# Keeping the running sum of a depthwise convolution in two PSUM banks, with the sample rows' products moved ahead of the taps

## What is computed

```python
h = xn @ w_in + b_in
a, gate = jnp.split(h, 2, axis=-1)
u = a * jax.nn.sigmoid(gate)
upad = jnp.concatenate([hist, u], axis=1)          # hist: 30 earlier rows (zero for the prompt)
y = depthwise_conv(upad, w_dw) + b_dw              # 31 taps, each channel by itself
y = jax.nn.silu(layernorm(y, ln_g, ln_b))
out = y @ w_out + b_out
```

## Time and profile before

| what | value |
| --- | --- |
| time, median of 3 runs | 3446.14 us (3438.42 to 3453.7) |
| span of the profiled execution | 3441.0 us (no time of its own is given beside the span) |
| TensorE busy | 2972.1 us, 86% |
| VectorE busy | 1332.7 us, 39% |
| ScalarE busy | 994.2 us, 29% |
| GpSimd busy | 971.2 us, 28% |
| mean granted TensorE clock | 0.926 of full speed |

### The profile page before, as it was taken

How to read it: one execution, slowest core, us unless ns; L and a number is a source line. 1 busy time by engine, 2 the same in 40 slices (tenths; PEclk the granted TensorE clock), 3 DMA queues, 4 the chain that set the end, 5 groups by cost and what they waited for, 6 DMA issues and landing times.

```text
span 3441.0 us, 49665 instructions
## 1 busy us (share of the span) xinstructions
PE 2972.1 (86%) x17970; PEld 2775.7 (81%) x17970; DVE 1332.7 (39%) x2005; ACT 994.2 (29%) x1549; POOL 971.2 (28%) x436
## 2 busy tenths in 40 slices
PE   5535336999999999989999999899898999999998
PEld 4535335889999999979997777778797999999997
DVE  6999996421111111251113555555334111111114
ACT  4323225232111111221113544455423211111113
POOL 2757571222212121231110000055613122222221
PEclk9767667999999999999996999988789999999998
DMA  3000000111111111122411201377511111111111
GB/s 95 19 24 12 24 12 20 43 37 40 52 40 46 43 43 49 37 68 82 121 39 31 70 25 25 101 254 262 195 43 37 40 46 43 40 52 34 52 36 70
DMA packets 243747, 206.54 MB, mean 60 GB/s; under 512 B 18252, under 2 KB 218956, under 8 KB 243652
## 3 DMA queue, kind: packets, MB, share of 16 engines
q1 hardware_dynamic: 230535, 186.66, 17.8%
q10 hardware_dynamic: 13133, 18.80, 1.6%
HBM read 183.16 MB, written 23.13 MB: 60 GB/s over the span
## 4 chain that ended last, share of the span: by engine, by line
PE 72%; DVE 15%; issue 7%; ACT 3%; DMA 1%; POOL 1%; DVEq 0%; ACTq 0%; SPq 0%; POOLq 0%
PE PS L706 19%; PE PS L708 18%; PE PS L707 18%; DVE yacc L1644 8%; PE PS L964 4%; PE PS L990 3%; PE PS L948 2%; DVE tm L1506 2%; PE PS L1027 1%; DVE rs L1485 1%; PE PS L1068 1%; PE PS L1040 1%; PE PS L1069 1%; PE PS L1041 1%; ACT pr L1394 1%
## 5 line engine op out<-in xcount | busy, mean ns | idle before, releaser
L706 PE MATMUL PS<-xhi,whi 128*128 128x352 f32 x3456 | 1144.4, 331 | 269.0 <-DVE u L1608 188.3
L708 PE MATMUL PS<-xlo,whi 128*128 128x352 f32 x3456 | 1122.3, 325 | 0.0
L707 PE MATMUL PS<-xhi,wlo 128*128 128x352 f32 x3456 | 1121.0, 324 | 0.0
L622 POOL TENSOR_TENSOR wlo<-wraw,whi 128x1024 fp32r<-128x1024 f32 x208 | 510.7, 2456 | 1608.4 <-ACT whi L1136 1608.4
L706 PEld LDWEIGHTS PS<-xhi,whi 128*128 128x128 f32 x3456 | 657.5, 190 | 311.6 <-DVE u L1608 190.3
L707 PEld LDWEIGHTS PS<-xhi,wlo 128*128 128x128 f32 x3456 | 660.9, 191 | 0.0
L708 PEld LDWEIGHTS PS<-xlo,whi 128*128 128x128 f32 x3456 | 658.6, 191 | 0.0
L1543 DVE TENSOR_TENSOR ht<-PS,ht 128x352 f32<-128x352 f32 x132 | 69.1, 525 | 908.4 <-PE PS L708 904.4
L1136 ACT ACTIVATE whi<-wraw 128x1024 fp32r<-128x1024 f32 x208 | 218.8, 1052 | 595.2 <-PE PS L708 567.2
L706 PE MATMUL PS<-hhi,whi 128*128 128x352 f32 x1056 | 341.2, 323 | 8.8 <-issue 8.8
L707 PE MATMUL PS<-hhi,wlo 128*128 128x352 f32 x1056 | 338.5, 321 | 0.0
(11 more groups left out here) (197 smaller groups left out, 3036.5 us busy)
## 6 DMA issues: line engine op xcount, KB each, us to landing
wraw<-in_ffn_w_gu SPq DMA_DIRECT2D x88, 512.0 KB, 3.8
kr<-in_cache_k SPq DMA_DIRECT2D x64, 512.0 KB, 4.8
vr<-in_cache_v SPq DMA_DIRECT2D x64, 512.0 KB, 4.8
wraw<-in_ffn_w_down SPq DMA_DIRECT2D x32, 384.0 KB, 3.4
wraw<-in_attn_w_in SPq DMA_DIRECT2D x24, 512.0 KB, 3.9
wraw<-in_ffn_w_down SPq DMA_DIRECT2D x32, 320.0 KB, 3.1
wraw<-in_conv_w_in SPq DMA_DIRECT2D x16, 512.0 KB, 3.8
wraw<-in_conv_w_out SPq DMA_DIRECT2D x8, 512.0 KB, 4.0
```

Of the source, the lines that this page charges most:

```text
L622: nc.gpsimd.tensor_tensor(wlo[:, s, :], wraw[:, s, :], whi[:, s, :].bitcast(F32), ALU.subtract).then_inc(w_lo, 1)
L706: nc.tensor.matmul(out, wh, hi[:, k, blk(b)], start=(k == 0), stop=False)
L707: nc.tensor.matmul(out, wl, hi[:, k, blk(b)], start=False, stop=False)
L708: m = nc.tensor.matmul(out, wh, lo[:, k, blk(b)], start=False, stop=(k == kc - 1))
```

## The change

```diff
-        yacc = at("yacc", [P, SEQ], F32, after("uprod"))
-        ys = at("ys", [P, NS], F32, after("yacc"))
+        ys = at("ys", [P, NS], F32, after("uprod"))
...
+        yacc = banks(6, SEQ)
...
-                step(nc.vector.tensor_scalar(yacc[:, :], u[:, 0:SEQ], wc[:, R_DW:R_DW + 1],
+                for t in range(TNEW):
+                    step(nc.vector.tensor_tensor(
+                        up[:, :, t, :], us[:, :, t:t + KW],
+                        wc[:, R_DW:R_DW + KW].rearrange("p (a k) -> p a k", a=1).broadcast_to([P, NREQ, KW]),
+                        ALU.mult))
+                products = n[0]
+
+                step(nc.vector.tensor_scalar(yacc, u[:, 0:SEQ], wc[:, R_DW:R_DW + 1],
                                              wc[:, R_BDW:R_BDW + 1], ALU.mult, ALU.add))
+                stepped(products)
+                step(nc.vector.tensor_reduce(ys[:, :], uprod[:, :, :], AX.X, ALU.add))
                 for k in range(1, KD):
                     have = n[0]
-                    if k <= TNEW:
-                        t = k - 1
-                        step(nc.vector.tensor_tensor(
-                            up[:, :, t, :], us[:, :, t:t + KW],
-                            wc[:, R_DW:R_DW + KW].rearrange("p (a k) -> p a k", a=1).broadcast_to([P, NREQ, KW]),
-                            ALU.mult))
-                    if k == TNEW + 2:
-                        step(nc.vector.tensor_reduce(ys[:, :], uprod[:, :, :], AX.X, ALU.add))
-                    if k == TNEW + 4:
+                    if k == 2:
                         step(nc.vector.tensor_scalar(
                             ycv[:, ds(c, 1), SEQ:T].rearrange("p a t -> p (a t)"), ys[:, :],
                             wc[:, R_BDW:R_BDW + 1], None, ALU.add))
 
                     stepped(have)
-                    step(nc.vector.scalar_tensor_tensor(yacc[:, :], u[:, k:k + SEQ], wc[:, R_DW + k:R_DW + k + 1],
-                                                        yacc[:, :], ALU.mult, ALU.add))
+                    step(nc.vector.scalar_tensor_tensor(yacc, u[:, k:k + SEQ], wc[:, R_DW + k:R_DW + k + 1],
+                                                        yacc, ALU.mult, ALU.add))
                 stepped(n[0])
...
-                nc.vector.tensor_tensor(ycv[:, ds(c, 1), 0:SEQ].rearrange("p a t -> p (a t)"), yacc[:, :], yp[:, :],
+                nc.vector.tensor_tensor(ycv[:, ds(c, 1), 0:SEQ].rearrange("p a t -> p (a t)"), yacc, yp[:, :],
```

## The result

The changed kernel takes 3292.58 us (median of 4 runs, 3282.46 to 3315.26) against 3449.44 (4 runs, 3438.42 to 3453.7): a ratio of 0.9567, 95% interval 0.9526 to 0.9608. The forecast was 3287.5 (3259 to 3325). A run in which TensorE is granted a lower clock is longer, and the ratios here leave out the slow runs, while medians and single times include them. The profiled spans differ by 3441.0 - 3280.7 = 160.3 us; the forecast was 158.6.

The account below looks back on a forecast made before the run. VectorE, its taps stretched beside GpSimd, was taken to bound the convolution loop. Terms sum to 35.4 us a turn instead of 55.86, 159 us saved over eight turns: 3446.1 - 158.6 = 3287.5 us, range 3259 to 3325.

Parts of the forecast that it names:

- The test row: VectorE subtraction of SBUF from PSUM, 1215 to 1226 ns beside GpSimd: with one input in PSUM neither engine waits.
- Four products: Convolution turn, products moved ahead of the taps and before GpSimd starts: 1.32 us for four.
- L1634 to the next start: Multiplication by the first weight, now written to PSUM: 1.20 us to the next start, bounds 0.72 and about 1.20.
- Reduction: Moved ahead of tap 1, which now waits for its end: 1.21 us a turn.
- Tap 1: First tap of a turn, after the moved reduction: 1.19 us to the next start.
- L1641: Small 32-wide bias addition, still SBUF only, to keep its price: 2.31 less 0.08 us, bounds 0.1 and 2.5.
- Taps 2 to 19: Main term, taps summing in PSUM: 1.335 us from tap to tap, 23.99 us a turn.
- The end of a turn: Final sum, then the steps to the next turn's first u block: 2.23 us, same price as before.
- GpSimd did not stay slow: Rival: GpSimd's additions stay at 3.14 us in the loop; about 40 us a turn, 3321 us, chance 6%.
- a second pass in place: Rival: in-place PSUM taps run at half rate, 20.3 us more a turn; 3446 us, no change, chance 4%.
- The third rival: Taps reading u from SBUF still collide with GpSimd: 58.0 us a turn, 17 us slower, 3463 us, chance 7%.
- theory A: VectorE instructions with two SBUF tensor inputs collide with GpSimd; those with a PSUM input do not.

Follow-up runs that it names:

- the order alone: The kernel before with only the new instruction order, the running sum kept in SBUF: 3471.6 us, ratio 1.0017 to the kernel before.
- the alternating sums: Taps alternate between a sum in PSUM and one in SBUF, odd taps reading PSUM and writing SBUF, even taps the reverse: 3380.91 us, one run.
- the one with the bias in the sum: The changed kernel without its small bias addition, the bias summed by the reduction as a 32nd column: ratio 0.9592 to the kernel before.

## Why the prediction was right

*The test row.* L1821 carried the forecast, and the taps did what it did: 1290 ns with GpSimd working. The question that it left open (its SBUF tile is the second input) is settled by these taps themselves: there the SBUF tile u is the first input, and a scalar pointer stands beside it, and they are not hit either.

*The terms.* Four products 1.31 us (1.32 in the sum). L1634 to the next start 1.25 (1.20): its 1.34 us lies above the upper bound taken from L1852, the only term outside its bounds, 0.4 us in all. Reduction 1.21 (1.21). Tap 1 1.20 (1.19). L1641 2.06 (2.23). Taps 2 to 19 23.80 (23.99). The end of a turn, with its 0.24, 2.23 (2.23). In all 35.13 against 35.4. GpSimd's additions ended 29.50 us after u (29.5), its subtractions 34.12 (34.3). (The sum gives 159 us, the forecast's last line subtracts 158.6.)

*Luck.* The turn and the loop (161.4 us against 159) test the working. That the whole time came within 5 us is partly luck: the four runs spread over 33 us, and the two profiles happened to have the same time behind the loop, 2914 and 2913 us. The 5 us by which the median before stood above the span were scatter, not an offset: each later run's time is 1.7 to 1.8 us above its own span.

*The Trainium skill against the row.* The 65 ns more per instruction, estimated in the prediction from the Trainium skill ("VectorE: DVE Perf Modes", section on the TRN2 errata), did not come: a tap is 1290 ns in PSUM and 1285 undisturbed in SBUF, 5 ns, as L1529 and L1548 had it. As for the same page's advice to copy to SBUF first (Rules for kernel authors of the Trainium skill): the run with the order alone keeps the sum there and has none of the gain.

*The rivals.* GpSimd did not stay slow (2.39 us an addition), nor is there a second pass in place. The third rival's sum was tried with the order alone and came out at no change instead of 17 us slower; it had the first two collisions and the multiplication by the first weight too long, as told above.

*What was not tried.* That banks 6 and 7 lie apart from TensorE's banks is part of this kernel; nothing was run in which both engines use one bank.

## What to carry to other kernels

Where VectorE and GpSimd work side by side, look at the min and max of one shape: two lengths meant a collision here, and among instructions with two tensor inputs those with both in SBUF were hit. (Small ones with a single input can be hit as well, see below.) Keeping one operand of a long chain in free PSUM banks frees both engines; moving the hit instructions ahead of GpSimd's start pays only where what then runs beside GpSimd cannot be hit: 17.8 us with the sum in PSUM, 1 us with it in SBUF. Before counting a gain in full, look for the engine that ends next: here GpSimd ended 0.67 us before VectorE's next turn.

## What the runs showed beyond that

A tiny SBUF-to-SBUF instruction can cost a whole GpSimd instruction: a bias on 32 columns takes 0.24 us alone and up to 2.4 beside GpSimd, a copy of 42 columns 0.19 and up to 1.8 (with the alternating sums). Both have a single tensor input, so theory A does not cover them. The reduction, which also reads one SBUF tensor and writes SBUF, takes 1.17 us beside GpSimd and is not hit; no run here shows what sets the two kinds apart.

The time behind the loop, the same 16674 TensorE instructions in each kernel, follows the granted clock of the run. It is 2913 us at 0.96 before, and in the profiles of all these kernels it grows as the clock falls. The two ends are the changed kernel and the one with the bias in the sum, both of the last session:

```profile
366.70:3263.10 2896.40, 2717.21 (x16674) 2542.55 (x16674) 848.25 (x1647) 834.50 (x1356) 660.22 (x308) 0.97 0.21 66
...
358.40:3336.40 2978.00, 2811.78 (x16674) 2615.41 (x16674) 848.43 (x1647) 834.57 (x1356) 660.65 (x308) 0.93 0.21 64
```

82 us lie between them, ten times what the experiment was after. What lowers the clock in a run is not settled here. A change in one stage is read from that stage.
